# A two-block transformer kernel on one core: other buffers for the rotations, other places for the weight splits and for a few dense pieces in two attention mixers

## The reference, cut to what matters

```python
def second_block(x, p, norm_g, ...):
    for i in range(DEPTH):                                   # DEPTH = 2
        h = h + 0.5 * rms_norm(swiglu(rms_norm(h, g[0]), ...), g[1])
        hn = rms_norm(h, g[2])
        if mixer == 0:                                       # layer 0: "mixer A"
            y = dilated_mixer(hn, a_wqkv[j], a_wo[j], cos, sin)
        elif mixer == 1:                                     # layer 1: "mixer B"
            y = window_gqa_mixer(hn, b_wqkv[j], b_wo[j], b_sink[j], cos, sin)
        h = h + rms_norm(y, g[3])
        ...
# both mixers: qkv = h @ wqkv; q, k = apply_rope(q), apply_rope(k)   (a rotation of 16 of 64 features)
#   A: 3 groups of 8 heads, distances 64, 256 and 1024 with dilations 1, 4 and 16
#   B: 16 query heads on 4 key heads, a band of 128 tokens to either side, and a sink logit
#   s = q k^T / 8, masked; softmax; o = p v; y = o @ wo
```

## Time and profile before

| | us |
|---|---|
| three runs, median (lowest to highest) | 3411.93 (3410.92 to 3412.04) |
| profiled execution | 3409.56 |
| its span, first to last instruction | 3407.7 |
| PE busy / DVE / ACT / POOL | 3335.2 / 1837.6 / 1241.5 / 336.2 |
| mixer A's attention and projection, about | 1690 to 1973 |
| mixer B's, about | 2794 to 2971 |

### The profile page before, as it was taken

How to read it: one execution, slowest core, us unless ns; L and a number is a source line. 1 busy time by engine, 2 the same in 40 slices (tenths; PEclk the granted TensorE clock), 3 DMA queues, 4 the chain that set the end, 5 groups by cost and what they waited for, 6 DMA issues and landing times.

```text
span 3407.7 us, 43209 instructions
## 1 busy us (share of the span) xinstructions
PE 3335.2 (98%) x16908; PEld 2657.2 (78%) x16908; DVE 1837.6 (54%) x2936; ACT 1241.5 (36%) x1878; POOL 336.2 (10%) x240
## 2 busy tenths in 40 slices
PE   9999999999999999999999999999999999999998
PEld 6767888776688887888777778888788876788886
DVE  5766334567753436443566664435644367654436
ACT  3354223424442324232333342224523235532324
POOL 0310000213100010000132200000000002100001
PEclk9999999999999999999999999999999999999999
DMA  4102222321122222223322222232222321122232
GB/s 163 63 32 75 93 99 99 123 68 44 57 81 98 94 99 81 98 98 104 114 69 69 69 81 92 99 105 97 85 96 98 105 95 40 61 101 96 99 105 81
DMA packets 81434, 300.40 MB, mean 88 GB/s; under 512 B 9040, under 2 KB 9040, under 8 KB 80640
## 3 DMA queue, kind: packets, MB, share of 16 engines
q1 hardware_dynamic: 78624, 284.20, 24.7%
q0 software_dynamic: 1568, 11.98, 0.9%
q10 hardware_dynamic: 1088, 2.10, 0.2%
HBM read 296.14 MB, written 2.10 MB: 88 GB/s over the span
## 4 chain that ended last, share of the span: by engine, by line
PE 88%; DVE 6%; ACT 3%; issue 1%; POOL 1%; DMA 1%; ACTq 0%; DVEq 0%; POOLq 0%
PE bank L879 25%; PE bank L881 25%; PE bank L880 25%; PE bank L923 2%; PE bank L924 2%; PE bank L930 2%; DVE wl L2054 1%; ACT sc L1738 1%; PE bank L1433 1%; PE bank L1445 1%; PE bank L1193 1%; PE bank L1174 1%; PE bank L1488 1%; PE bank L1132 1%; DVE sc L2345 1%
## 5 line engine op out<-in xcount | busy, mean ns | idle before, releaser
L879 PE MATMUL bank<-x,wh 128*128 128x512 f32 x2632 | 1052.9, 400 | 16.5 <-DVE h L2498 5.7
L881 PE MATMUL bank<-x,wl 128*128 128x512 f32 x2632 | 1026.8, 390 | 0.0
L880 PE MATMUL bank<-x,wh 128*128 128x512 f32 x2632 | 1025.7, 390 | 0.0
L1577 ACT ACTIVATE wh<-raw 128x1024 fp32r<-128x1024 f32 x528 | 558.1, 1058 | 1151.9 <-PE bank L881 1086.6
L2054 DVE TENSOR_TENSOR wl<-raw,wh 128x1024 fp32r<-128x1024 f32 x528 | 675.7, 1281 | 544.2 <-ACT wh L1577 543.0
L879 PEld LDWEIGHTS bank<-x,wh 128*128 128x128 f32 x2632 | 494.6, 188 | 137.5 <-issue 30.6
L881 PEld LDWEIGHTS bank<-x,wl 128*128 128x128 f32 x2632 | 494.4, 188 | 105.2
L880 PEld LDWEIGHTS bank<-x,wh 128*128 128x128 f32 x2632 | 495.3, 188 | 98.0 <-issue 3.4
L879 PE MATMUL bank<-mid,wh 128*128 128x512 f32 x1216 | 474.9, 391 | 0.5 <-DVE wl L2054 0.5
L881 PE MATMUL bank<-mid,wl 128*128 128x512 f32 x1216 | 473.1, 389 | 0.0
L880 PE MATMUL bank<-mid,wh 128*128 128x512 f32 x1216 | 473.1, 389 | 0.0
(11 more groups left out here) (349 smaller groups left out, 3338.8 us busy)
## 6 DMA issues: line engine op xcount, KB each, us to landing
raw<-stream SPq DMA_DIRECT2D x528, 512.0 KB, 3.3
raw_apart<-stream SPq DMA_DIRECT2D x10, 512.0 KB, 3.6
sm<-small POOLq DMA_DIRECT2D x2, 2144.0 KB, 10.6
tb<-tab POOLq DMA_DIRECT2D x2, 1728.0 KB, 14.8
h<-x_t ACTq DMA_DIRECT2D x4, 512.0 KB, 6.8
out_t<-h SPq DMA_DIRECT2D x8, 256.0 KB, 2.1
tba<-tab_a POOLq DMA_DIRECT2D x1, 1152.0 KB, 8.0
pf<-p_t POOLq DMA_DIRECT2D x2, 512.0 KB, 5.2
```

Of the source, the lines that this page charges most:

```text
L879: pe.matmul(dst, hi, src[:, kc, 0, :], start=start, stop=False)
L880: pe.matmul(dst, hi, src[:, kc, 1, :], start=False, stop=False)
L881: return pe.matmul(dst, lo, src[:, kc, 0, :], start=False, stop=stop)
L1577: act.activation(high_of(n)[:, :], raw_of(n)[:, :], ACT.Copy).then_inc(hi_done, 1)
```

## The change

In mixer A: ACT now does two splits at the end of tile 3 and none at the end of tile 35, so that in between, at the end of tile k, it does the high part of unit k+4. DVE does the same unit as before (k+3), but ahead of the tile's eviction and no longer behind it. Steps 5 and 9 have one dense piece fewer, so two pieces are left for the end. In both mixers the rotations go through four buffers (`prod` and `tmp`), not two. In mixer B 43 pieces, not 38, stand ahead of the first scores; the 13 matmuls are gone; `norm` 0 comes ahead of `scores` 1; DVE evicts tile 4 behind `norm` 0, and splits behind `scores` 0 and behind that eviction; and a step has as many pieces as it has key blocks (2, 3, 3, 2), not 2 in every third step and 3 in the others.

```diff
@@ plan_a
-        n = (6, 6, 6) if s < 11 else (5, 5, 4) if s == 11 else (2, 2, 2)
+        n = (6, 6, 5 if s in (5, 9) else 6) if s < 11 else (5, 5, 4) if s == 11 else (2, 2, 2)
@@ plan_b
-    yield from dense.send(38)
+    yield from dense.send(43)
     yield "scores", 0
-    yield from dense.send(2)
+    yield "exps", 0
+    yield from dense.send(3)
+    yield "norm", 0
     yield "scores", 1
-    yield "exps", 0
-    yield from dense.send(2)
     yield "exps", 1
-    yield "norm", 0
-    yield from dense.send(2)
+    yield from dense.send(3)
...
-        n = 3 if s % 3 else 2
-        if len(b_blocks(s)) == 3:
+        n = len(b_blocks(s))
+        if n == 3:
@@ POOL rope, DVE roped and roped_whole
+        turned_in = [prod[0], prod[1], tmp[0], tmp[1]]
-                rt = prod[k % 2][:, :]
+                rt = turned_in[k % 4][:, :]
-                if k >= 2:
-                    dve.wait_ge(rotated, k - 1)
+                if k >= 4:
+                    dve.wait_ge(rotated, k - 3)
@@ PE mixer_b
-                        if k == 0:
-                            stay_awake_in_next(13)
@@ ACT mixer_a, stage unit
-                        split_after(k, AFTER_NORM)
+                        split({0: 0, 2: 0, 3: 2, A_NEED - 1: 0}.get(k, 1))
@@ DVE mixer_a, stage unit
+                        if 3 <= k < A_NEED:
+                            split()
                         if k < A_NEED:
...
-                            split_after(k, AFTER_NORM)
+                        if k == 1:
+                            split()
@@ DVE mixer_b
+                def evict(k):
+                    unit_over()
...
+                    if stage == "unit" and k != 4:
+                        evict(k)
+                        if k < len(B_TILES) and k not in (0, 2, 3):
+                            split()
...
                         scores_b(k)
+                        if k == 0:
+                            split()
...
                         norm(k, 16, lambda g: b_scores(k, g))
+                        if k == 0:
+                            evict(4)
+                            split()
```

More of the change, by code:

```diff
@@ L2583, in roped @@
                 k = c.n.get("roped", 0)
-                if k >= 2:
-                    dve.wait_ge(rotated, k - 1)
-                dve.stream_shuffle(view(prod[k % 2][:, :]), src, SWAP)
+                if k >= 4:
+                    dve.wait_ge(rotated, k - 3)
+                dve.stream_shuffle(view(turned_in[k % 4][:, :]), src, SWAP)
                 free(dve.tensor_tensor(dst, src, cos, ALU.mult))
@@ L2713, in mixer_b @@
                 c.start(banks_mixer)
-                for stage, k in plan_b():
[L2715 to L2725, removed]
+                def evict(k):
+                    unit_over()
+                    if k < len(B_TILES):
+                        src = bank[c.peek()][:, :]
+                        if B_TILES[k][0] == "v":
+                            free(dve.tensor_tensor(bvs[:, :], src, rs_in[:, :], ALU.mult))
+                        elif k < 3:
+                            roped_whole(b_home(k)[:, :], src)
+                        else:
+                            roped(b_home(k)[:, :], src, tbb[:, B_COS:B_COS + S], lambda ap: ap)
+                for stage, k in plan_b():
+                    if stage == "unit" and k != 4:
+                        evict(k)
+                        if k < len(B_TILES) and k not in (0, 2, 3):
+                            split()
                     elif stage == "part":
```

## The result

The changed kernel took 3426.53 us (median of 6 runs, 3425.48 to 3429.14), the kernel before on the same chip 3410.98 (3410.14 to 3412.04): a ratio of 1.0048, 95% interval 1.0038 to 1.0059. That is 15.6 us slower, 1.4 above the predicted 3425.1. The profiled execution took 3426.83 us with a span of 3424.7, 17.0 more than before.

The account below looks back on a forecast made before the run. PE, busy for 3335.2 of 3407.7 us, was taken as the bound. Mixer A +11.8, B's start +0.9 and B later +0.5 gave +13.2 us on 3411.93, so 3425.1 us, range 3418 to 3431.

Parts of the forecast that it names:

- A, ScalarE one unit ahead: Mixer A: ScalarE waits 3.4 us for a load, delaying copies; tiles 16, 17, 25, 26 cost 2.7, 1.9, 1.2, 2.6 us.
- A, VectorE: Mixer A: splits ahead of evictions delay v tiles; tiles 7, 8, 34 cost 1.2, 0.5, 0.5 us, sum 2.2.
- Rival 1: Mixer A: PE nowhere waits for ScalarE's copies, VectorE's order still costs; +6.0 in all, 3417.9 us; chance 0.10.
- A, the start: Start of mixer A: scores 0 still wait for GpSimd's six rotations; gain 0.2 us, bounds gain 2.0, loss 0.5.
- A, the end: From mixer A's last values to projection: VectorE's split, hidden before, now stands behind PE's last piece; +1.4 us.
- B, the start: Start of mixer B: VectorE late, PE idle 5.0 us ahead of values 0, 3.2 ahead of group (1,0); net +0.9.
- B, later: Later steps of mixer B: 6.2 us PE work against 8 of VectorE where tiles end; +0.5, bounds -0.7 and +1.5.
- the third rival: Mixer B: clock falls to half once or twice behind idle, each stretch costing 1.7 us; 3427 to 3429 us, chance 0.10.
- Rival 2: Loads land within about 1.9 us, all aimed waits in A and B go: -11.9 us, 3400 us; chance 0.07.

Follow-up runs that it names:

- experiment 1: Changed kernel with mixer A's splits put back as before on both engines, the rest of the change kept: 3418.22 us, ratio 1.0026.
- experiment 4: Kernel before with only VectorE's split put ahead of the eviction in mixer A, from tile 3 on: 3421.97 us, ratio 1.0035.
- Experiment 10: Kernel before with the changed mixer B and four buffers, but two-block steps giving three pieces and three-block steps two: 3410.84 us, ratio 1.0002.
- experiment 3: Kernel before with only ScalarE one unit ahead in mixer A, VectorE still splitting behind its eviction: 3423.73 us, ratio 1.0041.
- Experiments 7: Kernel before with the change of mixer B and the four buffers, mixer A's order as before: 3414.65 us, ratio 1.0014.
- 8: Kernel before with changed mixer B and four buffers, plus 15 dummy matmuls ahead of TensorE's 4.1 us wait in B: 3414.73 us, ratio 1.0014.
- experiments 5: Kernel before with only two dense pieces, from steps 5 and 9 of mixer A, kept for its end: 3413.77 us, ratio 1.0013.
- experiment 6: Kernel before with two pieces kept for mixer A's end, but issued behind the low halves of the output: 3411.23 us, ratio 1.0003.

## Why the prediction came out right

The sign came out by the mechanism. The size came out partly by luck, by terms that cancel. Mixer A was predicted at 11.8 us and took 13.4 more, of which 9.3 are idle time; mixer B was predicted at 1.4, at most 3.0 by its bounds, and took 6.2 more, of which 2.6 are idle time. In idle time the prediction had 13.2 us; the mixers show 9.3 + 2.6 = 11.9. In longer busy time it had nothing; the mixers show 7.7, at most 7.0 of it by half clock, and 2.8 us are given back elsewhere.

- **A, ScalarE one unit ahead: right in mechanism.** Tile 16: predicted 2.7, measured 2.44. Tile 17: 1.9 against 1.53 (0.65 at the turn, 0.88 at the values). Tile 26: 2.6 against 2.28 (0.21 at the turn, 2.07 at the values). Tile 25: 1.2 against 0.81 (0.21 at the turn, 0.60 at group 2). The load landed after 3.2 us, not 3.4, which is a part of it; the rest I have not traced.
- **A, VectorE: right at tile 7 (1.2 against 1.37 - 0.29 = 1.08)**, 0.21 at tile 8 against 0.5. At tile 34 PE waited 0.46 us for VectorE's copy, near the predicted 0.5, but that is luck: in experiment 1, without these splits, it waits 0.85 there. Rival 1's sum left this tile's 0.5 out. I had taken the two engines' parts as sums with prices of their own, ScalarE's 8.4 and VectorE's rest. The two came to 10.6; by experiment 1 the splits cost 10.2, but only 6.6 of it as idle time; longer busy time, which I had not counted, made up the rest. As prices of the parts it was wrong: experiment 4 shows 12.7 for VectorE's alone. With ScalarE as before, VectorE's order would have cost nearly as much as both.
- **A, the start: right.** Scores 0 came 0.56 us earlier (predicted 0.2), and they began 0.06 us behind the last rotation (1709.42 + 1.29 and 1710.77):

```profile
1708.06 1.28 POOL L811 TENSOR_TENSOR prod<-prod,tba 128x512 f32<-128x512 f32 x1
1709.42 1.29 POOL L812 TENSOR_TENSOR aq<-aq,prod 128x512 f32<-128x512 f32 x1
```

The reason held too: five of the twelve rotation rows take over 2.1 us, as before. The gain goes with the four buffers: scores 0 start 46.1 to 46.2 us into A in every run that has them, and 46.7 to 46.8 in every run with two, whatever the order of the splits.

- **A, the end: right.** +1.4 predicted, 3.10 - 1.64 = 1.46 measured. Step 12: 0 predicted; 1.27 and 0.46 us of waits in place of 1.02.
- **B, the start: right in sum, each wait too large.** 5.0 and 3.2 predicted, 4.08 and 1.88 measured. Group (1,0) began 48.22 us into B, 44.71 before, with 3.4 us of pieces more done: +0.1 against the predicted 0.9 (which took 2822.5 where the chain ahead of it gave 2822.4).
- **B, later: the term that was mis-sized.** It was 0.5 us for "a last and a first step of a head pair" at two tiles, upper bound 1.5. Measured are five waits of 0.74, 0.69, 0.98, 1.38 and 0.76, 4.55 in all against 0.77 before: 3.8. Experiment 10 shows the pattern of the pieces to be 2.3 of it; that they are five fewer is left for the rest, and no run shows it by itself.
- **The clock: the third rival, at 0.10, came true, and wider than it was put.** It named B only; B had one stretch of 10.2 us (3.6 us of busy time, against 1.7 to 3.4), A two of 3.4. Its total of 3427 to 3429 lay near the 3426.5 measured since idle time was smaller by 1.3 and other stretches of the kernel were 2.8 shorter.
- **Rival 2** failed where it was said to: the load landed 3.2 us after its issue, not 1.9.

What stands open is why the parts ahead of A and behind B were 2.8 us shorter: the stretches at half clock there come and go from kernel to kernel with no edit near them, and 1.1 us of idle time went that I have not traced.

## What to carry to other kernels

Work for a later unit may go ahead of work for this one only if its inputs are there: an in-order engine that waits for a load holds up whatever short copy stands behind it, and one that puts its split ahead of a short job inherits the wait for the other engine's half. Filler for a waiting engine is not free because its sum is constant: in this kernel waits opened in the steps that it was taken from. Giving the pieces out so that the steps were equally long took back 2.3 of 3.8 us in one kernel and little in the other, so try that first, and then look at the waits again. And with an engine that has no slack, price an idle of 2 to 3 us at more than its length, because of the clock.

## What the runs showed of the hardware

**The clock fell behind shorter idles than I had taken, and not behind all.** It fell to half at 1868.6 behind an idle of 2.07 us, and in experiment 3 behind idles of 2.59 and 2.31; but it stayed at 1.00 behind 2.44 us at tile 16, and before behind 3.06 us in B. Experiments 7 and 8 have the same code in mixer A and the same idle of 1.96 us ahead of scores 0. These are the stretches behind it, in 7 and in 8:

```profile
1712.90:1716.30 3.40, 3.40 (x15) 2.55 (x12) 1.84 (x7) 0.00 (x0) 0.00 (x0) 0.50 0.00 0
```

```profile
1714.70:1718.10 3.40, 3.40 (x22) 2.68 (x19) 2.35 (x9) 1.03 (x1) 0.00 (x0) 1.00 0.03 10
```

A took 314.55 us in 7 and 313.47 in 8. So the length of the idle alone doesn't decide. The Trainium skill (TensorE: Matmul & The Clock Gate, "Why this matters for your kernels") warns of idle between bursts; a figure for how much is safe can't be had from these runs.

**What such a stretch costs could be measured on code that no edit had touched.** In experiments 5 and 3 mixer B was that of before and idled as before (5.6 us), but the clock was at half in it for 3.4 and 6.8 us. The third row is experiment 6, where it stayed at 1.00:

```profile
2776.50:2975.90 199.40, 193.75 (x1158) 136.95 (x1158) 150.80 (x402) 105.24 (x235) 34.26 (x21) 0.99 0.16 54
```

```profile
2786.10:2986.60 200.50, 194.92 (x1158) 137.79 (x1158) 150.67 (x402) 105.05 (x235) 34.24 (x21) 0.98 0.16 54
```

```profile
2774.10:2972.00 197.90, 192.25 (x1158) 136.13 (x1158) 150.71 (x402) 105.13 (x235) 34.24 (x21) 1.00 0.16 54
```

1.5 us for 3.4 at half clock and 2.7 for 6.8. It also means that two single profiles can differ by 2.6 us in a mixer whose code is the same: compare idle and busy time apart, not lengths.

**GpSimd's rotations take less time where VectorE's splits are out of their way.** It was busy for 88.94 us in A before and 72.54 after with the same 52 instructions, and 73.43 in experiment 4, which changes VectorE's order alone; with the four buffers and VectorE's old order it was 89.17 (experiment 1). It shortened no wait that I could find: only scores 0 wait for the rotations, and their start goes with the buffers.
